# The decay matrices of a state space mixer, built from one row product per head over both halves of the tokens

## The reference, cut to what matters

```python
def segsum_exp(a):
    cs = jnp.cumsum(a, axis=-1)
    diff = cs[..., :, None] - cs[..., None, :]
    return jnp.where(mask, jnp.exp(jnp.where(mask, diff, 0.0)), 0.0)   # mask: lower triangle

a = dt * A                                   # per token and head, negative
Lmat = segsum_exp(a)                         # decay from token s to token l
CB = jnp.einsum('bclgn,bcsgn->bcgls', Cc, Bc)
y_diag = jnp.einsum('bcgls,bgrcls,bcsgrp->bclgrp', CB, Lmat, X)
```

## Time and profile before

| | us |
|---|---|
| runs of the kernel | 986.51, 986.75, 989.81 |
| median | 986.75 |
| the profiled execution | 986.9 |
| its span in the trace | 985.0 |

### The profile page before, as it was taken

The page is one execution under the profiler, slowest core; times in us unless marked ns, Lnnn a source line. Parts: engine busy times, 40 slices in busy tenths (PEclk is TensorE's granted clock), DMA queues, the critical chain, the costliest instruction groups (busy, mean ns, idle before and its releaser), DMA issues.

```text
span 985.0 us, 15897 instructions
## 1 busy us (share of the span) xinstructions
PE 964.7 (98%) x6552; PEld 872.4 (89%) x6552; DVE 631.7 (64%) x822; ACT 507.9 (52%) x746; POOL 52.5 (5%) x88
## 2 busy tenths in 40 slices
PE   7999999999999999999999999999999999999996
PEld 5877889989999888998988899998998899999995
DVE  5766676676655555777867687775554556555544
ACT  5564655555544444566645574544455454444442
POOL 3000001002000000300000002100100020000000
PEclk9999999999999999999999999999999999999999
DMA  8974345564666555465554546464755446565651
GB/s 274 314 239 121 112 125 139 171 193 152 210 196 190 179 185 189 122 204 158 183 160 126 150 138 200 154 195 128 235 161 160 128 151 204 181 197 175 196 182 43
DMA packets 135079, 170.36 MB, mean 173 GB/s; under 512 B 7664, under 2 KB 99104, under 8 KB 135008
## 3 DMA queue, kind: packets, MB, share of 16 engines
q1 hardware_dynamic: 133472, 165.47, 54.9%
q10 hardware_dynamic: 992, 2.58, 0.8%
q0 software_dynamic: 544, 1.31, 0.5%
HBM read 168.28 MB, written 1.05 MB: 172 GB/s over the span
## 4 chain that ended last, share of the span: by engine, by line
PE 90%; DVE 5%; ACT 3%; issue 1%; DMA 1%; DVEq 0%; POOLq 0%; POOL 0%; SPq 0%; ACTq 0%
PE ps L357 14%; PE ps L359 13%; PE ps L358 13%; PE ps L387 7%; PE ps L389 7%; PE ps L388 7%; PE ps L694 5%; PE ps L695 5%; PE ps L693 5%; PE ps L340 5%; PE ps L436 3%; DVE parts L1404 2%; PE ps L467 1%; PE ps L469 1%; PE ps L468 1%
## 5 line engine op out<-in xcount | busy, mean ns | idle before, releaser
L1404 DVE TENSOR_TENSOR parts<-raws,parts 128x1024 fp32r<-128x1024 f32 (+1 forms) x308 | 367.7, 1211 | 235.4 <-ACT parts L953 234.9
L953 ACT ACTIVATE parts<-raws 128x1024 fp32r<-128x1024 f32 (+1 forms) x308 | 315.4, 1043 | 243.6 <-PE ps L359 135.9
L357 PE MATMUL ps<-room_r,parts 128*128 128x256 f32 x1248 | 352.6, 283 | 0.9 <-DVE parts L1404 0.9
L359 PE MATMUL ps<-room_r,parts 128*128 128x256 f32 x1248 | 348.7, 279 | 0.0
L358 PE MATMUL ps<-room_r,parts 128*128 128x256 f32 x1248 | 348.4, 279 | 0.0
L357 PEld LDWEIGHTS ps<-room_r,parts 128*128 128x128 f32 x1248 | 234.6, 188 | 7.1 <-issue 3.9
L358 PEld LDWEIGHTS ps<-room_r,parts 128*128 128x128 f32 x1248 | 234.7, 188 | 1.3
L359 PEld LDWEIGHTS ps<-room_r,parts 128*128 128x128 f32 x1248 | 234.6, 188 | 0.0
L387 PE MATMUL ps<-parts,room_r 128*128 128x512 f32 (+1 forms) x336 | 136.2, 405 | 2.6 <-DVE parts L1404 2.6
L389 PE MATMUL ps<-parts,room_r 128*128 128x512 f32 (+1 forms) x336 | 132.2, 393 | 0.0
L388 PE MATMUL ps<-parts,room_r 128*128 128x512 f32 (+1 forms) x336 | 132.2, 393 | 0.0
(11 more groups left out here) (191 smaller groups left out, 841.4 us busy)
## 6 DMA issues: line engine op xcount, KB each, us to landing
raws<-in_w_in SPq DMA_DIRECT2D x100, 512.0 KB, 3.9
raws<-in_w_ffn_in SPq DMA_DIRECT2D x44, 512.0 KB, 4.5
raws<-in_w_up SPq DMA_DIRECT2D x32, 512.0 KB, 4.4
raws<-in_w_down SPq DMA_DIRECT2D x32, 512.0 KB, 4.3
raws<-in_w_ffn_out SPq DMA_DIRECT2D x22, 512.0 KB, 4.2
raws<-in_w_xkv SPq DMA_DIRECT2D x16, 512.0 KB, 4.4
raws<-in_w_out SPq DMA_DIRECT2D x8, 512.0 KB, 4.1
raws<-in_w_up_ssd SPq DMA_DIRECT2D x8, 512.0 KB, 5.1
```

What stands on the lines that cost most here:

```text
L357: e.matmul(ps, wh, hT[0][:, k, :], start=k == 0, stop=False)
L359: last = e.matmul(ps, wl, hT[0][:, k, :], start=False, stop=k == K - 1)
L953: e.activation(t.h, t.raw, ACT.Copy).then_inc(s["hi"], 1)
L1404: e.tensor_tensor(t.l, t.raw, t.h.bitcast(F32), ALU.subtract).then_inc(s["lo"], 1)
```

## The change

The decay matrix is made in another way. One column vector of a per head is summed up along the tokens by a product with `upper`, which gives a matrix `cs` with the heads in rows 0 to 15 and the tokens of both halves in 256 columns. The same sums stand once more in rows 32 to 47. `cs` is rounded to fp32r (ACT), and rows 32 to 47 are replaced by the rest that the rounding left (DVE, 16 partitions). `sel` has ones at rows n and n+32 in column n, in fp32r; the product of one of its columns, spread by a stride of zero over 128 columns, with `cs` puts cs[l] of head n into all 128 partitions, for both halves at once. ACT subtracts that from cs[s] (a bias per partition) with Relu, one head and half at a time, and takes exp(-x) of it. The heads are taken four at a time for both halves (q = 0 to 3). `seg_in` and La are gone; E has four buffers.

```diff
-        rot = [chunks(f32(8192 + 512 * i, 512), 4) for i in range(6)]
-        La, E = rot[0:3], rot[3:6]
-        quads = [(t, q) for t in range(2) for q in range(4)]
+        decays = [chunks(f32(9216 + 512 * i, 512), 4) for i in range(4)]
+        E = lambda t, q: decays[2 * (q % 2) + t]
...
 PE:
-            group(psum[:, b, 0:16], [(upper, a3[:, 1, :])])
-            ends(group(psum[:, b, 16:32], [(after, a3[:, 0, :])]), "dec", b)
+            group(psum[:, b, 0:32], [(upper, a3)])
+            ends(group(psum[:, b, 32:48], [(after, a3[:, 0, :])]), "dec", b)
+            b = bank()
+            need(s["a_twice"], 1)
+            for t in range(2):
+                last = group(psum[:, b, t * P:t * P + P], [(twice[:, t, :], upper)])
+            ends(last, "cs", b)
             step()
...
-            def seg(i):
-                b = bank()
-                need(s["La"], i + 1)
-                for h in range(4):
-                    last = group(psum[:, b, h * P:h * P + P], [(La[i % 3][:, h, :], upper)])
-                ends(last, ("seg", i), b)
+            def seg(q):
+                out_of("cs")
+                need(s["sel"], 1)
+                for i in range(2):
+                    b = bank()
+                    for h in range(2):
+                        n = 4 * q + 2 * i + h
+                        last = group(psum[:, b, 256 * h:256 * h + 256], [(sel[:, n:n + 1].to_broadcast([P, P]), cs)])
+                    ends(last, ("seg", q, i), b)
...
             seg(0)
-            seg(1)
-            step(5)
-            for i in range(8):
-                if i + 2 < 8:
-                    seg(i + 2)
+            step(4)
+            for q in range(4):
+                if q < 3:
+                    seg(q + 1)
                 step()
-                diag(i)
-                if i < 6:
-                    step()
-                if i in (2, 4, 6):
-                    y_out(*((0, 0), (0, 1), (1, 0))[i // 2 - 1])
+                if q == 2:
+                    y_out(0, 0)
+                diag(0, q)
+                step()
+                if q == 2:
+                    y_out(1, 0)
+                diag(1, q)
+                step(2 if q < 3 else 1)
+            y_out(0, 1)
             step(3)
             y_out(1, 1)
...
 ACT:
-            full("dec")
-            step(e.activation(e1, psum[:, where["dec"].bank, 0:16], ACT.Exp))
-            emptied(e.activation(d0, psum[:, where["dec"].bank, 16:32], ACT.Exp), "dec")
+            full("cs")
+            e.activation(cs, psum[:, where["cs"].bank, 0:256], ACT.Copy).then_inc(s["cs_hi"], 1)
+            step(e.activation(sums_, psum[:, where["dec"].bank, 0:32], ACT.Copy))
+            step(e.activation(e1, psum[:, where["dec"].bank, 16:32], ACT.Exp))
+            emptied(e.activation(d0, psum[:, where["dec"].bank, 32:48], ACT.Exp), "dec")
+            settle()
...
-                emptied(e.activation(E[i % 3], chunks(psum[:, where["seg", i].bank, :], 4), ACT.Exp), ("seg", i))
+            def seg(q):
+                if q >= 2:
+                    until(where["diag", 1, q - 2].at)
+                    e.wait_ge(s["pe"], where["diag", 1, q - 2].at)
+                for i in range(2):
+                    full(("seg", q, i))
+                    v = psum[:, where["seg", q, i].bank, :].rearrange("p (h t n) -> p h t n", h=2, t=2)
+                    for t in range(2):
+                        for h in range(2):
+                            n = 4 * q + 2 * i + h
+                            inst = e.activation(E(t, q)[:, 2 * i + h, :], v[:, h, t, :], ACT.Relu,
+                                                bias=sums3[:, t, n:n + 1], scale=-1.0)
...
+                settle()
+                for t in range(2):
+                    out_of(("seg", q, 1))
+                    e.activation(E(t, q), E(t, q), ACT.Exp, scale=-1.0).then_inc(s["decays"], 1)
...
 DVE:
             conv(3)
+            step(e.memset(twice, 0.0))
+            tt(sel, ident[:, 0:16], ident[:, 32:48], ALU.add).then_inc(s["sel"], 1)
...
             e.wait_ge(s["a"], 1)
+            e.tensor_copy(twice[:, :, 32:48], a3).then_inc(s["a_twice"], 1)
...
-            seg_in(0)
-            seg_in(1)
             (X of both halves, as before)
-            until(where["dec"].at)
+            until(where["cs"].at)
+            rows_ = slice(32, 48)
+            e.wait_ge(s["cs_hi"], 1)
+            emptied(tt(cs[rows_, :], bank_of("cs")[rows_, 0:256], cs[rows_, :].bitcast(F32), ALU.subtract), "cs")
             out_of("dec")
...
-                ts(y, y, yrs[:, j:j + 1], ALU.mult).then_inc(s["y_out"], 1)
+            def y_scaled(t, g):
+                y, n = xs[:, t, 512 * g:512 * g + 512], 2 * g + t
+                e.wait_ge(s["y_rstd"], n + 1)
+                ts(y, y, yrs[:, n:n + 1], ALU.mult).then_inc(s["y_out"], 1)
...
             seg(0)
+            for q in range(4):
+                if q < 3:
+                    seg(q + 1)
+                if q % 2:
+                    y_part(0, q // 2)
+                    y_part(1, q // 2)
+                    y_scaled(0, q // 2)
+                    y_scaled(1, q // 2)
+                if q == 2:
+                    for t in range(2):
+                        y_T(t, 0)
+            for t in range(2):
+                y_T(t, 1)
```

More of the change, by code:

```diff
@@ L47 @@
     "ret_sq", "ret_rstd", "ret", "oT_hi", "retT_hi", "gates", "mix", "mix_hi", "mixT", "up", "up_hi", "upT",
-    "pad", "conv_in", "conv", "silu", "gated", "Aexp", "dt", "soft_e", "soft", "soft_exp", "a", "X", "Xd", "La", "E",
+    "pad", "conv_in", "conv", "silu", "gated", "Aexp", "dt", "soft_e", "soft", "soft_exp", "a", "a_twice", "sel", "cs_hi", "decays", "X", "Xd", "E",
     "y_sq", "y_sum", "y_rstd", "y_out", "yT_gain", "yT_hi", "yT", "la", "la_min", "la_ln", "bcum", "bexp", "qt", "kt",
@@ L222, in build @@
         small = r2.take(256)
-        dt_, e_, s_, s2_, p_, aa = (small[:, 32 * i:32 * i + 32] for i in range(6))
+        dt_, e_, s_, s2_, p_, sums_ = (small[:, 32 * i:32 * i + 32] for i in range(6))
         Aexp, e1, d0 = (small[:, 192 + 16 * i:208 + 16 * i] for i in range(3))
         dt3 = dt_.rearrange("p (t h) -> p t h", t=2)
-        a3 = aa.rearrange("p (t h) -> p t h", t=2)
+        twice = f32(8192, 256).rearrange("p (t c) -> p t c", t=2)
+        a3 = twice[:, :, 0:16]
+        sums3 = sums_.rearrange("p (t h) -> p t h", t=2)
+        cs, sel = room_r[:, 8448:8704], room_r[:, 8704:8720]
         at_zs = r2.at
@@ L771, in tensor, with diag @@
                 ends(group(psum[:, b, 256:384], [(cv[:, 8 + g, P:256], cv[:, 10 + g, P:256])]), ("CB", g), b)
-            def seg(i):
-                b = bank()
-                need(s["La"], i + 1)
-                for h in range(4):
-                    last = group(psum[:, b, h * P:h * P + P], [(La[i % 3][:, h, :], upper)])
-                ends(last, ("seg", i), b)
[L780 to L784, removed]
+            def seg(q):
[7 more added lines that the diff above has]
+                    ends(last, ("seg", q, i), b)
+            yb = [None, None]
+            def diag(t, q):
                 g = q // 2
                 if q % 2 == 0:
-                    yb = bank()
-                need(s["E"], i + 1)
+                    yb[t] = bank()
+                need(s["E"], 2 * q + t + 1)
                 need(s["X"], t + 1)
@@ L791, in diag @@
                     o = 256 * (q % 2) + 64 * h
-                    last = group(psum[:, yb, o:o + 64], [(E[i % 3][:, h, :], X[:, t, 256 * q + 64 * h:256 * q + 64 * h + 64])])
+                    last = group(psum[:, yb[t], o:o + 64],
+                                 [(E(t, q)[:, h, :], X[:, t, 256 * q + 64 * h:256 * q + 64 * h + 64])])
                 if q % 2 == 0:
-                    where["diag", i] = Group(None, done(last), None)
+                    where["diag", t, q] = Group(None, done(last), None)
                     return
-                ends(last, ("y", t, g), yb)
-                where["diag", i] = where["y", t, g]
+                ends(last, ("y", t, g), yb[t])
+                where["diag", t, q] = where["y", t, g]
                 if t:
@@ L804, in y_out @@
             def y_out(t, g):
[L805 removed]
+                need(s["y_out"], 2 * g + t + 1)
                 turn(("yT", t, g), [xs[:, t, 512 * g + P * j:512 * g + P * j + P] for j in range(4)])
             seg(0)
[L809 to L819 removed]
+            step(4)
+            for q in range(4):
+                if q < 3:
+                    seg(q + 1)
+                step()
+                if q == 2:
[7 more added lines that the diff above has]
+            y_out(0, 1)
             step(3)
@@ new lines, in scalar @@
+            e.activation(cs, psum[:, where["cs"].bank, 0:256], ACT.Copy).then_inc(s["cs_hi"], 1)
[15 more added lines that the diff above has]
+                                                bias=sums3[:, t, n:n + 1], scale=-1.0)
+                            if t and h:
```

(33 more changed lines are left out.)

8 lines of the change are left out of this document (1 added, 7 removed).

## The result

The changed kernel takes 991.64 us (median of 22 runs, 988.24 to 993.71), the kernel before in the same comparison 987.54 (986.28 to 990.10, 22 runs). The ratio is 1.0036, interval 1.0025 to 1.0046: slower by 3.6 us. (The two medians differ by 4.1; the times of each kernel lie in clusters, and a median can fall between two of them.) The profiled execution took 990.1 with a span of 988.2; before it was 986.9 and 985.0.

What follows compares the result with a forecast made beforehand. PE, busy 98% of the span, was taken to bound the kernel. Terms -4.7 + 0.1 + 2.8 + 1.7 + 1.7 gave +1.6 us, hence 988.4 us (chance 0.43) from a median of 986.75; range 983.5 to 990.5.

Steps and rivals of the forecast that it cites:

- PE's own work: PE in the edited stage: seg quads removed -7.0, row products +1.9, cs +0.4, sum -4.7 us.
- (a): At cs, PE waits 0.1 us for DVE's copy `a_twice`.
- (b): Before seg(0), PE waits 2.8 us for DVE to write the rest of cs, behind X; bounds 2.4 and 3.2.
- (c): Behind the wait at seg(0), PE's clock falls to half, +1.7 us; bounds 0 and 1.7 for each such wait.
- Rival 1: The clock stays up behind both waits, no fall: 986.8 us; chance 0.27.
- (d): At y_out(0,1), PE waits 1.7 us for DVE, which does y_part(1,1) ahead of y_scaled(0,1); bounds 0.5 and 2.5.
- The cover of ACT's longer chain: From seg(q) to diag(0,q): 11 to 14 us of PE steps cover the 7 us chain, so no cost.
- rival 4: ACT reloads its table between Relu and Exp, 10.3 us of ACT, still covered: 988.5 us; no chance of its own.
- Sum: All terms over the whole kernel: -4.7 + 0.1 + 2.8 + 1.7 + 1.7 = +1.6 us.
- Rivals 2 and 3: 2: DVE in time, no waits that count, 982.2 us, chance 0.14; 3: row products not single-pass, 993.7 us, chance 0.07.

Runs made afterwards that it cites:

- e9: e3 with e5, on the changed kernel: both cs and seg(0) later and DVE's rounding behind y; 982.67 us, ratio 0.9952 to the kernel before.
- e6: The kernel of e4 with the row products done as plain fp32, not in a single pass; 988.31 us, ratio 1.0008 to the kernel before.
- e10: The kernel of e5 again, unchanged, timed in 12 executions; 987.74 us, ratio 0.9994 to the kernel before.
- e5: Changed kernel, but behind the last quad DVE takes the second half's y and yx before its rounding for the weight tile; one execution, 986.48 us.
- e1: Changed kernel, but PE issues y_out(0,1) two steps later, three steps behind yx; 987.02 us, ratio 0.9992 to the kernel before.
- e3: Changed kernel, but PE makes cs behind the first step and issues seg(0) two steps later; 987.92 us, ratio 0.9999 to the kernel before.
- e4: Changed kernel with the edits of e1 and e3 together; 983.88 us, ratio 0.9968 to the kernel before.
- e2: Changed kernel, but DVE multiplies the first half's y by its factor before starting on the second half; 985.80 us, ratio 0.9976 to the kernel before.
- e7: Changed kernel with the edits of e3 and e2 together; 985.48 us, ratio 0.9972 to the kernel before.
- e8: The kernel of e4 with the products of la issued one step later; 986.44 us, ratio 0.9985 to the kernel before.

## Why the prediction was right or wrong

- **PE's own work, -4.7**: right. e9 is 4.81 under before with the waits gone, and e6 shows the single pass in it: without it 4.7 to 5.1 us come back, where the rows gave 5.2.
- **(a), 0.1**: wrong in kind. `a_twice` did not matter, but PE waited 1.92 us right there: cs takes one PSUM bank more, and the next free one was still being emptied by ACT, which copied z out at 472.13. The prediction never asks which bank cs gets and who empties it.
- **(b), 2.8 in front of seg(0)**: the mechanism was right (X, then the rest of cs at 477.89, PE at 478.36), the size 0.68, because (a)'s wait had already made PE late. Together they are 2.6, against 2.9 in the sum: the total came out near by luck, from two errors of opposite sign.
- **(c), the clock**: it fell once, as forecast, for 1.7 us, but behind y_out(0,1) and not behind seg(0). Rival 1 is out for the profiled execution. e10 shows that a fall at the start can come too. The prediction took the wait at 92 us for the only one of its size; the kernel before has another, 1.94 us at 11.2 us, with no fall behind it.
- **(d), 1.7, bounds 0.5 to 2.5 at y_out(0,1)**: this is the step that failed. It was 3.3. That PE would wait there for DVE's factor was right; the term was too small, since it let DVE's rounding start as soon as yx ended. The prediction named the two copies of r and then set them off against an earlier skip term. In fact ACT's square, its two copies and its rounding stood in one row, and DVE's rounding behind them; so the rounding began 1.75 us later than in the sum, which covers the missing 1.6. e5 takes the rounding out of the row and the wait goes to zero.
- **The cover of ACT's longer chain**: right. Eight Relu are 2.16 us and two Exp 1.15, 0.27 and 0.57 apart, where 0.29 and 0.6 were taken from the mean durations in the earlier trace rows; ACT's busy time grew by 8.7 us against the 9.3 for the Relu. No table load came between (rival 4), and PE waited for E nowhere.
- **Sum**: -4.7 + 2.6 + 3.3 + 1.7 = +2.9 against +1.6; 3.07 was measured from the transposes, 3.6 by the ratio. The range (983.5 to 990.5) was set about a median of 986.75 from three runs, which more runs put at 987.54. That 0.8 and the 1.3 by which the terms came out higher lift 988.4 to 990.5, the edge of the range, and the profiled execution, 990.1, is inside it. The last 1.1 us to 991.64 are in executions that were not profiled: 12 of the 22 have spans from 989.6 to 991.6 us with mean granted clocks of 0.990 to 0.994. Where their clock fell isn't on record, so this part stays open. A second fall, which the prediction's bounds named, was left out of its range.

Rivals 2 and 3 did not come: there were waits, and the row products took 4 instructions a pack, not 8. The waits at the start and at y_out are separate causes: e1, e3 and e4 remove 3.6, 3.1 and 6.6 us.

Where the 1.3 to 1.7 us at the weight tile near 577 us come from can be followed one step back. Behind y_out come the products of la, which the edit doesn't touch. DVE takes them out of PSUM. Their start on PE and the start of DVE's instructions on them, before and in e4:

```profile
557.03 1.99 PE L340 MATMUL ps<-room,wa 16*128 16x256 f32 x8
558.85 1.66 DVE L1441 TENSOR_SCALAR room<-ps,cols 128x256 f32<-128x256 f32 x4
...
552.56 1.99 PE L345 MATMUL ps<-room,wa 16*128 16x256 f32 x8
555.82 1.66 DVE L1481 TENSOR_SCALAR room<-ps,cols 128x256 f32<-128x256 f32 x4
```

DVE comes 1.8 us behind PE before, in the changed kernel, e3, e5 and e9, but 3.3 in e4, 3.2 in e1 and 2.9 in e2 and e7. These 1.0 to 1.4 us are what the weight tile waits more. In e1 and e2 DVE finishes the last factor 79.3 us behind the transposes of xs, as late as in the changed kernel, while PE is 5 us ahead of its course there; in e5 it is 76.0. Which instruction of DVE's queue would have to move to free e1 and e2 wasn't tried.

## What to carry to other kernels

A saving on the bound engine is only had if nothing that feeds it is issued later or in another order: read, for each product that is moved, the last thing in front of its input in the other engines' queues, roundings and copies for other work included, and which PSUM bank it gets and who empties it. Where two independent halves are finished in one go, let the first one's result out before starting the second, or keep the filler's housekeeping out of the chain between them. And look at the clock behind a wait of PE: behind the 3.3 us wait at y_out(0,1) the fall cost 1.7 us more, behind the 1.9 us wait for cs in e10 0.6.

## What the runs showed of the hardware that was not expected

The same wait isn't always followed by a fall of the clock. The 2.24 us in front of the transposes near 91 us (in the earlier trace rows, followed by a fall) stand in all twelve profiles. Near their end the clock fell, at 91 to 93 us, in both kernels, e1, e4, e6 and e9. In e2 it fell neither there nor anywhere until the end. In e3, e5, e7, e8 and e10 it had fallen at 12 us, behind a wait of 2.0 to 2.3 us for the first weight tile (1.9 us in the others), and fell again at 101 us, in the next wait or just behind it. In e2 this wait reads:

```profile
99.81 0.66 PE L441 MATMUL ps<-ident,big 128*128 128x128 f32 x4 [2.65 <-DVE big L1476]
```

Behind the 3.3 us at y_out(0,1) it fell in both profiles that have that wait (the changed kernel and e3), for 3.4 us each time. The falls at 101 us lasted 3.4 us in e3 and e5, and 6.8 in e7, e8 and e10.

A fall cost nothing where PE waited for another engine right after it: e1 (fall at 91 us, then a wait of 1.10) and e2 (no fall, 2.65) both go on at 99.81 us. At 101 us there is no such wait: from there to the transposes of xs it is 367.4 us in both kernels and in e1, e2, e4, e6 and e9, 368.9 and 369.0 in e3 and e5, and 370.2 to 370.4 in e7, e8 and e10. That is up to 2.9 of the 4.6 us by which the stage moves between profiles. Between 110 and 970 us no profile has a fall but those at y_out(0,1) and, in e10, behind cs, so the early falls are not in the column from the transposes to the end.

It fits the spread of the runs: the changed kernel's spans go from 986.3 us with a mean granted clock of 0.994 to 0.995 to 991.6 with 0.990, and half a percent of the clock over 990 us is 5 us.
